# Dense gates through indirect DMA additions in DRAM in place of one-hot products, in an encoder layer with product-key experts

## What is computed

```python
# h: (1024, 1024) after RMSNorm and modulation
q = (h @ w_q).reshape(T, 8, 2, 128)                  # 8 heads, 2 halves
s = einsum('thpd,hpnd->thpn', q, sub_keys)           # 2 x 128 scores a head
vals, idx = top_k(s, 16)
cand = vals[:, :, 0, :, None] + vals[:, :, 1, None, :]
top_s, top_pos = top_k(cand.reshape(T, 8, 256), 16)
experts = i1 * 128 + i2                              # 128 experts a token, of 16384
gates = softmax(top_s)                               # 16 gates a head
y = sum_e gates_e * gelu(u[expert_e] . h) * v[expert_e]
x = x + gate2 * rmsnorm(y)
```

## Time and profile before

| | |
|---|---|
| median of 3 runs | 2855.0 us (2849.57 to 2856.36) |
| profiled execution, span from first to last instruction | 2847.3 us |
| its own device time | not shown apart; the median of the runs is 7.7 us above the span |
| PE busy | 2774.5 us, 97% of the span |
| DVE, ACT, POOL busy | 76%, 44%, 46% |
| mean granted TensorE clock | 0.992 of full speed |
| bytes moved | 721 MB, 253 GB/s on average |

### The profile page before, as it was taken

How to read it: one execution, slowest core, us unless ns; L and a number is a source line. 1 busy time by engine, 2 the same in 40 slices (tenths; PEclk the granted TensorE clock), 3 DMA queues, 4 the chain that set the end, 5 groups by cost and what they waited for, 6 DMA issues and landing times.

```text
span 2847.3 us, 43522 instructions
## 1 busy us (share of the span) xinstructions
PE 2774.5 (97%) x15948; PEld 2538.1 (89%) x15948; DVE 2158.4 (76%) x3708; ACT 1249.3 (44%) x2302; POOL 1313.3 (46%) x1036
## 2 busy tenths in 40 slices
PE   6998999999999999999999999999999999999998
PEld 5776778889999999999999999999998887877786
DVE  7655545887668778678989898777768878887888
ACT  4333662233357767744454544445522233332233
POOL 0002000000000000177878887777778888888884
PEclk9998999999999999999999999999999999999999
DMA  7520223225556566589898999899999999999996
GB/s 281 227 71 31 89 75 111 69 78 177 182 177 211 200 203 205 185 286 316 301 329 301 314 303 331 308 331 311 321 361 380 359 333 345 374 341 356 341 358 262
DMA packets 328417, 721.37 MB, mean 253 GB/s; under 512 B 44000, under 2 KB 159840, under 8 KB 326368
## 3 DMA queue, kind: packets, MB, share of 16 engines
q1 hardware_dynamic: 238176, 451.18, 44.9%
q0 software_dynamic: 90112, 268.76, 27.3%
HBM read 605.50 MB, written 114.30 MB: 253 GB/s over the span
## 4 chain that ended last, share of the span: by engine, by line
PE 57%; POOL 18%; issue 5%; DVE 2%; ACT 1%; DMA 1%; DVEq 0%; SPq 0%; ACTq 0%; POOLq 0%
PE mix L1434 47%; POOL picked_act L1872 9%; POOL rows L1879 9%; PE mix L116 5%; PE sps_all L1929 2%; PE sps_all L1947 1%; PE mix L1947 1%; ACT onehot L1641 1%; PE sps_all L1521 1%; DMA rows<-in_v,eidx 0%; DVE lo L106 0%; DVE onehot L1723 0%; DMA wq_raw<-in_w_q 0%; DVEq L1123 0%; ACT hi L101 0%
## 5 line engine op out<-in xcount | busy, mean ns | idle before, releaser
L1872 POOL DMA_INDIRECT picked_act<-act_early,aidx x384 | 467.0, 1216 | 1043.0 <-PE mix L1434 938.5
L1434 PE MATMUL mix<-a_hi,hi 128*128 128x320 f32 (+1 forms) x3072 | 810.1, 318 | 2.0 <-DVE lo L106 1.9
L1434 PE MATMUL mix<-a_lo,hi 128*128 128x320 f32 (+1 forms) x3072 | 808.8, 317 | 0.0
L1434 PE MATMUL mix<-a_hi,lo 128*128 128x320 f32 (+1 forms) x3072 | 808.5, 317 | 0.0
L1879 POOL DMA_INDIRECT rows<-in_v,eidx x512 | 651.3, 1272 | 166.4 <-issue 133.2
L1782 DVE SCALAR_TENSOR_TENSOR ys<-rows,coef,ys 128x1024 f32<-128x1024 f32 x504 | 633.9, 1284 | 118.6 <-DMA rows<-in_v,eidx 105.3
L106 DVE TENSOR_TENSOR lo<-raw,hi 128x1024 fp32r<-128x1024 f32 x384 | 469.2, 1222 | 301.4 <-ACT hi L101 301.0
L101 ACT ACTIVATE hi<-raw 128x1024 fp32r<-128x1024 f32 x384 | 404.8, 1054 | 358.3 <-PE mix L1947 348.3
L1434 PEld LDWEIGHTS mix<-a_hi,hi 128*128 128x128 f32 x3072 | 533.6, 188 | 3.2 <-ACT gelu L1650 2.3
L1434 PEld LDWEIGHTS mix<-a_lo,hi 128*128 128x128 f32 x3072 | 535.1, 188 | 0.0
L1434 PEld LDWEIGHTS mix<-a_hi,lo 128*128 128x128 f32 x3072 | 534.7, 188 | 0.0
(11 more groups left out here) (268 smaller groups left out, 3899.3 us busy)
## 6 DMA issues: line engine op xcount, KB each, us to landing
raw<-in_u SPq DMA_DIRECT2D x256, 512.0 KB, 4.9
raw<-in_v SPq DMA_DIRECT2D x128, 512.0 KB, 6.0
act_late<-gelu SPq DMA_DIRECT2D x128, 320.0 KB, 4.6
act_in<-act_late SPq DMA_DIRECT2D x128, 256.0 KB, 6.5
act_early<-gelu SPq DMA_DIRECT2D x128, 192.0 KB, 1.8
gate_d<-free_lo SPq DMA_DIRECT2D x19, 1024.0 KB, 8.1
gt<-gate_d SPq DMA_DIRECT2D x64, 256.0 KB
free_lo<-gate_d SPq DMA_DIRECT2D x64, 256.0 KB, 7.6
```

What stands on the lines that cost most here:

```text
L1434: done = pe.matmul(dst, w, a[:, k, cols], start=first, stop=last)
L1872: pool.indirect_dma_start(out=g.picked_act[:, e:e + 1], out_offset=None, in_=act_tables[e // (EARLY * CHOSEN)], in_offset=bass.IndirectOff ...
```

## The change

The dense gates are no longer computed. A DRAM table `act_gates` has, for each expert, 512 activations and 512 gates in one row of 4 KB. SP fills the gate half with zeros (`clear_gates`, 8 DMAs of 4 MB, between the loads and stores of the first 8 retrieval tiles). POOL then adds each gate with an indirect DMA of one float for each of 128 tokens (`scatter_gates`, with an addition in the DMA): 4 dense tiles x 8 heads x 16 slots = 512 of them. Experts of one head are distinct, those of two heads may be the same, so all 16 additions of a head and tile have landed before the next head of that tile begins. POOL does them ahead of its first pick: first three tiles together, head by head, then the fourth tile alone.

For this the three tiles whose top-k is found in retrieval are now dense ones, and DVE finishes their gates and slots two heads at a time (`shift_heads`, `exp_heads` on ACT, `finish_heads`). The first of the five later tiles is the fourth dense one, and the other four are the gathered tiles. The early sweep is over token columns 640 to 1023, the late one over 0 to 639. In the dense sweep one load of 512 KB brings activations and gates of a block (`ag_in`). The schedule of picks and rows (`ROWS_FROM`, `ROW_EVERY`, `LEAD`) is the same.

```diff
-HEAD_TILES = EARLY
+HEAD_TILES = DENSE - 1
+HEAD_GROUP = 2
+HEAD_EXPS_AT = (7, 11, 15)
-TOPK_ORDER = (1, 2, 3, 4, 0)
+TOPK_ORDER = tuple(t - HEAD_TILES for t in (HEAD_TILES, *GATHERED_TILES))
-GATES_FROM, GATES_EVERY = 46, 3
+AG = 2 * DTOK
+ZERO_TILES = 16
...
+def finish_heads(g, dve, b):
+    gates = g.gates_d[:, 0:HEAD_TILES, group_heads(b), :]
+    norm = g.norm[:, 0:HEAD_TILES * HEAD_GROUP].rearrange("p (c h) -> p c h", h=HEAD_GROUP)
+    dve.wait_ge(g.heads_exps, b + 1)
+    dve.tensor_reduce(norm, gates, AX, ALU.add)
...
+       .then_inc(g.scatter_ready, 1)
...
+    def clear_gates(j):
+        tables = g.act_gates[j * ZERO_TILES:(j + 1) * ZERO_TILES, :, DTOK:].rearrange("n p c -> p n c")
+        sp.dma_start(tables, g.zeros[:].unsqueeze(1).to_broadcast([P, ZERO_TILES, DTOK])).then_inc(g.zeros_stored, 16)
...
+        if n < N // ZERO_TILES:
+            clear_gates(n)
         if n:
             store(n - 1)
...
+            if stage == 4 and h and h % HEAD_GROUP == 0:
+                finish_heads(g, dve, h // HEAD_GROUP - 1)
             head_stage(g, dve, h, stage)
+        if h % HEAD_GROUP == HEAD_GROUP - 1:
+            shift_heads(g, dve, h // HEAD_GROUP)
...
-        dve.tensor_tensor(pieces(g.cf[n % 2]), gates, pieces(g.act_in[n % ACTS]), ALU.mult)\
+        both = g.ag_in[n % ACTS]
+        dve.tensor_tensor(g.cf[n % 2][:], both[:, 0:DTOK], both[:, DTOK:], ALU.mult).then_inc(g.cf_ready, 1)
...
+    def scatter_gates(t, head):
+        if head:
+            pool.wait_ge(g.scattered[t], 16 * TOPK * head)
+        for k in range(TOPK):
+            pool.indirect_dma_start(out=gate_table, out_offset=bass.IndirectOffsetOnAxis(ap=g.sidx[:, t, head, k:k + 1], axis=0),
+                                    in_=g.gates_d[:, t, head, k:k + 1], in_offset=None, compute_op=ALU.add)\
+                .then_inc(g.scattered[t], 16)
+
+    pool.memset(g.zeros[:], 0.0).then_inc(g.zeros_ready, 1)
+    for head in range(HEADS):
+        if head == 0:
+            pool.wait_ge(g.zeros_stored, 16 * N // ZERO_TILES)
+        if head % HEAD_GROUP == 0:
+            pool.wait_ge(g.scatter_ready, head // HEAD_GROUP + 1)
+        for t in range(HEAD_TILES):
+            scatter_gates(t, head)
+    pool.wait_ge(g.scatter_ready, HEADS // HEAD_GROUP + 1)
+    for head in range(HEADS):
+        scatter_gates(HEAD_TILES, head)
     act_complete(N - 1)
     for e in range(GATHERED * CHOSEN):
...
-    def gates(b, later=0):
-        u = onehot_buffer(b)
-        pe.wait_ge(g.onehot_ready, 2 * (b + 1) + 2 * later)
-        if b:
-            pe.wait_ge(g.gate_out, b + later)
-        for t in range(BATCH):
-            last = pe.matmul(g.gps[:, t], g.onehot_1[u][:, t, :], g.onehot_2[u][:, t, :], start=True, stop=True)
-        last.then_inc(g.gate_ps, 1)
```

More of the change, by code:

```diff
@@ L44 @@
 DENSE = TT - GATHERED
+GATHERED_TILES = tuple(LATE + s if s < EARLY else DENSE + s - EARLY for s in range(GATHERED))
 DTOK = DENSE * P
-HEAD_TILES = EARLY
+HEAD_TILES = DENSE - 1
+HEAD_GROUP = 2
+HEAD_EXPS_AT = (7, 11, 15)
 STAGES = 4
@@ L1227, in token_numbers @@
         dve.tensor_scalar(g.token_col[:, s:s + 1], g.token_col[:, 0:1], float(s % EARLY * P), None, ALU.add)
+    for t in range(DENSE):
+        dve.tensor_scalar(g.gate_col[:, t:t + 1], g.token_col[:, 0:1], float(DTOK + t * P), None, ALU.add)
 def topk_turn(m):
@@ L1233, in topk_turn, with stores_of, acts_stored @@
     return (x, at) if m >= TOPK_FROM and x < TOPK_TILES else (None, None)
[L1236 to L1280, removed]
+def stores_of(m):
+    return 1 if m < N or LATE == DENSE else 2
+def acts_stored(last, s):
+    return 16 * sum(stores_of(m) for m in range(s, last + 1, GELUS))
 def rows_by(m):
@@ L1385, in load_raw, with load_act_gates @@
     sp.dma_start(g.raw[m % RAWS][:], src).then_inc(g.raw_in[m % RAWS], 16)
[L1388 to L1399, removed]
+def load_act_gates(g, sp, n):
+    sp.dma_start(g.ag_in[n % ACTS][:], g.act_gates[n]).then_inc(g.ag_in_sem[n % ACTS], 16)
 def split_expert_hi(g, act, m):
@@ L1424, in expert_product @@
     if m < N:
[L1425 removed]
+        parts = [(acc[:, 0:EARLY * P], slice(LATE * P, S))]
+    elif LATE * P <= HALF:
+        parts = [(acc[:, 0:LATE * P], slice(0, LATE * P))]
     else:
         wide = LATE * P // 2
[L1428 to L1429 removed]
+        parts = [(acc[:, half * HALF:half * HALF + wide], slice(half * wide, (half + 1) * wide)) for half in range(2)]
     for k in range(KC):
@@ L1548, in gathered_steps @@
             if m == last_row_at(s) + (1 if s < GATHERED - 1 else -3):
+                if s == 0:
+                    for t in range(DENSE):
+                        sp.wait_ge(g.scattered[t], 16 * CHOSEN)
                 if s < GATHERED - 1:
@@ L1647, in activate @@
         if m >= GELUS:
-            act.wait_ge(g.act_stored[m % GELUS], 16 * (m // GELUS))
+            act.wait_ge(g.act_stored[m % GELUS], acts_stored(m - GELUS, m % GELUS))
+        else:
+            act.wait_ge(g.zeros_stored, 16 * N // ZERO_TILES)
         if m < N:
             act.activation(g.gelu[m % GELUS][:, 0:EARLY * P], g.mps[m % 2][:, 0:EARLY * P], ACT.Gelu).then_inc(g.gelu_done, 1)
+        elif LATE * P <= HALF:
+            act.activation(g.gelu[m % GELUS][:, 0:LATE * P], g.mps[m % 2][:, 0:LATE * P], ACT.Gelu).then_inc(g.gelu_done, 1)
         else:
@@ L1736, in topk_steps @@
         pair, step = divmod(at, PAIR_STEPS)
-        gates = g.gates_a[:, x % 2]
+        gates = g.gates_of(x)
         if pair < PAIRS_OF_HEADS:
@@ L1953, in dense_product @@
             done.then_inc(g.tile_done, 1)
-    def key_steps(m):
-        expert_product(g, pe, m)
-        x, batch = gate_turn(m)
-        if x is not None and batch < 0:
-            transpose_slots(x)
-        elif x is not None:
-            gates(x * GATE_BATCHES + batch)
-    m = 1
-    while m < 2 * N:
-        rounds = key_rounds(m)
-        if rounds < 2:
-            key_steps(m)
-            m += 1
-            continue
-        with pe.Fori(0, rounds) as q:
-            for step in range(m, m + ROUND):
-                expert_product(g, pe, step, ROUND * q)
-                if gate_batch(step) is not None:
-                    gates(gate_batch(step), ROUND // GATES_EVERY * q)
-        m += rounds * ROUND
+    expert_product(g, pe, 1)
+    for first, last in ((2, N), (N, 2 * N)):
+        rounds = (last - first) // ROUND
+        with pe.Fori(0, rounds) as q:
+            for m in range(first, first + ROUND):
+                expert_product(g, pe, m, ROUND * q)
+        for m in range(first + rounds * ROUND, last):
+            expert_product(g, pe, m)
     dense_product(0)
```

243 lines of the change are left out of this document (85 added, 158 removed).

## The result

The changed kernel takes 3163.2 us (median of 4 runs, 3160.8 to 3171.2), the kernel before 2855.7 us on the same chip: ratio 1.109, 95% interval 1.107 to 1.111. It is slower by 308 us where 45 were forecast, outside the range of 2808 to 3030 us. The direction was right, and so was the chain of events; one price in it was not, and it carries nearly the whole error.

The account below looks back on a forecast made before the run. PE was taken to bound the kernel, 97% busy, with POOL's chain almost as long. -63 + 4 + 99 + 5 = +45 us on a 2847.3 us span, plus 7.7 for the median, gave 2900 us; range 2808 to 3030.

Parts of the forecast that it names:

- Taken from PE: Both sweeps: 64 gate batches and four groups of slot transposes gone, -63 us, 26 early and 37 late.
- Zeros in retrieval: Retrieval: stores of zeros lengthen the queue's work to 13.2 us in a 12.68 us period, +4 us, at worst +45.
- Additions at 1.41 us each: POOL ahead of its first pick: each addition priced as a pick, 1.25 us, plus 0.16 for DVE's share.
- The part for DVE: Additions, 630 to 826 us: DVE's two-input instructions fill 37% of the time and add 0.16 us to each.
- the seven landings: Fourth tile's additions: POOL waits seven times for the last 16 to land, 3 us each, 21 us.
- From floor 1.25 to 1.65: Range given for an addition's price on POOL: from an unhindered pick to a pick's pace in the dense sweep.
- POOL free at 1290 us: End of the additions: 548 + 541 + 180 + 21 us; first rows then come late and PE stands 99 us.
- Pace of the late sweep: Late sweep after the stall: rows at 7.0 to 7.15 us a block against 7.04, +5 us (0 to 12).
- the dense sweep (0): Dense sweep: gate multiplication stays one DVE instruction on 512 columns, 711 us as before, no change.
- the likeliest case: POOL comes free at 1250 to 1340 us: 2863 to 2955 us, 2900 in the middle; chance 0.42.
- An addition costs more than a pick: Rival: an addition also reads the table; 2947 us, or 3147 if POOL spends 1.89 us each; chance 0.16 for over 2955.
- POOL's place: Expert half: PE's blocks and POOL's indirect DMAs are two chains of almost the same length.

Follow-up runs that it names:

- the plain scatter: Changed kernel with all 512 additions written as scatters that replace the value in the table instead of adding to it: 3258.6 us, ratio 1.128.
- The moved additions: Changed kernel with all 512 additions, the fourth dense tile's 128 standing one behind each of the first 128 rows, not ahead of the first pick: 3184.1 us, ratio 1.115.

## Why the prediction was wrong, step by step

**Taken from PE (63 us): right.** The late sweep lost 35.5 us (37 forecast). The early one lost 22.9 (26) counted from its first gelu, 28.6 from its sixth: its first four steps took 4.8 to 6.1 us instead of 4.16. In the kernel before four of its first five steps take 4.5 to 5.2 us as well, and its first gelu comes late, only 1.3 us ahead of the second. The forecast had no term for either. The kernels without additions and without zeros have the same early sweep (533.9 and 533.8 us from first to last gelu), so neither the additions nor the zeros make the first blocks slow. What does stays open.

**Zeros in retrieval (+4, at worst +45): too low.** It was +11.1, of which the run without zeros gives back 9.4. The queue's mean load was reckoned, 13.2 us in a period of 12.7, but the load that matters is the one right behind a store. It cost nothing in the end: the first rows were wanted 10.5 us later for it and for the slower first blocks, and the stall is that much shorter.

**Additions at 1.41 us each: this is the step that failed.** They took 2.01 us. The part for DVE came out near in the sum: with the seven landings (11.9 us in all, 21 forecast) taken off, (1027.3 - 11.9)/512 = 1.98, so 1.98 - 1.85 = 0.13 us against 0.16. In part that is luck, for it was not spread as forecast: in the early sweep 254 additions fill 525 us, 2.07 each, 0.22 over 1.85, and the last 171, with DVE idle in PE's stall, had nothing to add. A place in the early sweep (start, us, of POOL and of DVE):

```profile
700.23 2.00 POOL L1836 DMA_INDIRECT act_gates<-gates_d,sidx  x1 [0.30 <-issue]
702.54 1.55 POOL L1836 DMA_INDIRECT act_gates<-gates_d,sidx  x1 [0.30 <-issue]
...
699.59 1.23 DVE L102 TENSOR_TENSOR lo<-raw,hi 128x1024 fp32r<-128x1024 f32 x1 [2.31 <-ACT hi L97]
...
703.75 1.23 DVE L102 TENSOR_TENSOR lo<-raw,hi 128x1024 fp32r<-128x1024 f32 x1 [1.55 <-ACT hi L97]
```

An addition that begins while a low part runs (here with 0.59 us of it left) takes 2.00 us. A low part that begins while an addition runs takes its usual 1.23 us, 127 times in the early sweep. The Trainium skill (SBUF — State Buffer, section Who interferes with whom, on the port pair that DVE and GpSimd share) says that the one that is later fully waits. The trace agrees for GpSimd as the later one; for DVE as the later one it shows no wait.

What was wrong is the floor under it. It was read off a pick, 0.95 + 0.30 = 1.25 us, and the addition's is 1.55 + 0.30 = 1.85. The 0.60 us, times 512, are 307 us, and the plain scatter's 0.95 shows that they belong to the addition alone; what GpSimd does in them no run shows. "From floor 1.25 to 1.65" were both bounds for DVE's share; the unknown instruction itself had none above. The prediction's remark that "descriptors of 4 bytes and of 4 KB cost POOL the same" compared two copies and said nothing of an operation with arithmetic.

**POOL free at 1290 us:** 1569 us, 279 later, and with it the stall of 363 instead of 99. The mechanism behind that time held: 25 us from there to TensorE's restart at 1594 us (31 forecast), one wait of DVE for a pick and one of PE for a low part, and POOL without a gap until its last row. The 2.2 us that the lower clock took at the restart had no term in the sum.

**Pace of the late sweep (+5) and the dense sweep (0):** 1.7 us and 5.9 us. The latter is not explained; PE's waits in it grew by 1.5 us, and the four runs of this kernel lie 10 us apart.

**The sum and its bounds.** The sum of 2892 us follows from its terms. The range of the likeliest case does not quite: POOL free at 1250 and at 1340 us gives 2860 and 2950 us by the same terms, not 2863 and 2955. Nothing hangs on it.

**The rivals.** "An addition costs more than a pick" had this very case, POOL spending half as much again on descriptors: 1.89 us each, free at 1537 us, 3147 us. It measured 2.01, 1569 and 3163. It was given part of a chance of 0.16, and the range ended at 3030, under it.

**What the forecast said of POOL's place:** "what is put ahead of POOL's first pick counts as much as what is taken from PE". The moved additions widen this. The loss is not that they stood ahead of the first pick; it is POOL's total.

## What to carry to other kernels

When an engine that idles early and is full late gets new work, ask for its total from the first moment at which it can start; below the free room (here some 320 additions by the estimate; 256 were measured to be free, 384 not) it is free, above it its time is in the kernel's, in both of the orders tried. And where the trace has no row for an operation, give its own price a top bound of its own, half as much again or more over the nearest relative, before contention is added; with 512 repetitions that bound is the range.

## What the runs showed of the hardware

An indirect transfer of 128 times 4 bytes costs GpSimd 0.95 us as a gather and as a plain scatter to DRAM, and 1.55 us as an addition in DRAM, with 0.30 us to the next; an addition lands after 3.0 us. The two kinds of scatter also differ on their way. The DMA view counts for the software queue, in the changed kernel (700 to 1100 us) and then in the one with plain scatters (600 to 664 us):

```profile
q0 software_dynamic: 27648, 0.11, 15.6%
...
act_gates<-gates_d,sidx POOLq DMA_INDIRECT x193
```

```profile
q0 software_dynamic: 1632, 0.03, 1.9%
...
act_gates<-gates_d,sidx POOLq DMA_INDIRECT x51
```

That is 27648/193 = 143 packets for each addition and 1632/51 = 32 for each plain scatter. The pages of whole executions give it without the edges of a window: 163840 packets with the 512 additions, 106496 with the 512 plain scatters and 90112 with neither, so 144 for each addition and 32 for each plain scatter. Such scatters in direct succession, every 1.26 us, went with a near stop of the issue of instructions on all other engines, in the one kernel and on the one chip where they were tried; with a MEMSET between two of them, or a drain and a MEMSET, each on another chip, nothing stopped. Neither the additions nor the picks and rows of any kernel here did it.
